# A third softmax buffer, with the softmax transposes and the value products one projection tile later

## What is computed

```
u = RMSNorm(h);  p = u @ w_in              # 28 column tiles of 128: rq rk rv rg dq dk dv, 4 heads each
# differential attention, head h, sequence b
logits = (q . k) * scale + bias            # two halves of 64 dims: two softmaxes, p0 and p1
a      = softmax(logits0) - lam * softmax(logits1)
out    = a @ v;  out = RMSNorm(out) * gain * (1 - lam_init)
# retention (second head group): scores * decay, times v, group norm, silu gate
h = h + concat(retention, attention) @ w_out
```

## Time and profile before

| what | before |
|---|---|
| median of 3 runs | 1997.98 us (1997.11 to 1999.52) |
| the profiled execution | 1998.23 us |
| its span in the trace | 1996.4 us, so 1.8 us lie around it |
| TensorE busy | 1955.0 us, 98% of the span, 8698 matmuls |
| VectorE, ScalarE, GpSimd busy | 732.5, 700.0, 856.0 us (37%, 35%, 43%) |
| mean granted TensorE clock | 0.993 of full speed |
| HBM traffic | 93 GB/s over the span |
| chain that ended last | TensorE 91%, VectorE 5%, issue 3%, ScalarE 1% |

### The profile page before, as it was taken

How to read it: one execution, slowest core, us unless ns; L and a number is a source line. 1 busy time by engine, 2 the same in 40 slices (tenths; PEclk the granted TensorE clock), 3 DMA queues, 4 the chain that set the end, 5 groups by cost and what they waited for, 6 DMA issues and landing times.

```text
span 1996.4 us, 24454 instructions
## 1 busy us (share of the span) xinstructions
PE 1955.0 (98%) x8698; PEld 1608.2 (81%) x8698; DVE 732.5 (37%) x1007; ACT 700.0 (35%) x997; POOL 856.0 (43%) x388
## 2 busy tenths in 40 slices
PE   9999999998899999999999999999989999999997
PEld 7888888886688888888878888888767888888886
DVE  4212332428575221212442124233485642122125
ACT  5322333445434322322532223234454243222224
POOL 4444443453334444444344444435433344444442
PEclk9999999999999999999999999999999999999999
DMA  4323232321122232222233222323211133222222
GB/s 149 130 98 114 96 110 90 100 97 62 49 68 86 97 103 96 95 95 93 91 103 117 95 95 95 105 82 109 85 53 53 53 106 105 96 95 95 95 95 74
DMA packets 54965, 186.00 MB, mean 93 GB/s; under 512 B 6440, under 2 KB 7976, under 8 KB 54860
## 3 DMA queue, kind: packets, MB, share of 16 engines
q1 hardware_dynamic: 53136, 181.61, 27.5%
q10 hardware_dynamic: 1724, 2.96, 0.5%
HBM read 182.44 MB, written 3.15 MB: 93 GB/s over the span
## 4 chain that ended last, share of the span: by engine, by line
PE 91%; DVE 5%; issue 3%; ACT 1%; DMA 0%; SPq 0%; DVEq 0%; ACTq 0%; POOL 0%; POOLq 0%
PE bank L457 20%; PE bank L459 20%; PE bank L458 20%; PE pair L457 7%; PE pair L459 7%; PE pair L458 7%; DVE neg_max L1184 1%; PE bank L479 1%; PE bank L475 1%; PE bank L476 1%; PE pair L672 1%; PE bank L687 1%; ACT s L933 1%; PE pair L506 1%; PE pair L501 1%
## 5 line engine op out<-in xcount | busy, mean ns | idle before, releaser
L415 POOL TENSOR_TENSOR w_lo<-raw,w_hi 128x1024 fp32r<-128x1024 f32 (+1 forms) x344 | 810.1, 2356 | 1088.4 <-ACT w_hi L745 1088.2
L745 ACT ACTIVATE w_hi<-raw 128x1024 fp32r<-128x1024 f32 (+1 forms) x344 | 355.5, 1034 | 680.3 <-PE bank L459 511.7
L457 PE MATMUL bank<-hg_hi,w_hi 128*128 128x512 f32 x1128 | 445.6, 395 | 0.0
L458 PE MATMUL bank<-hg_lo,w_hi 128*128 128x512 f32 x1128 | 440.6, 391 | 0.0
L459 PE MATMUL bank<-hg_hi,w_lo 128*128 128x512 f32 x1128 | 440.4, 390 | 0.0
L457 PE MATMUL bank<-a_hi,w_hi 128*128 128x512 f32 x768 | 299.5, 390 | 0.0
L458 PE MATMUL bank<-a_lo,w_hi 128*128 128x512 f32 x768 | 298.8, 389 | 0.0
L459 PE MATMUL bank<-a_hi,w_lo 128*128 128x512 f32 x768 | 298.8, 389 | 0.0
L457 PE MATMUL pair<-hg_hi,w_hi 128*128 128x512 f32 x656 | 255.2, 389 | 0.0
L458 PE MATMUL pair<-hg_lo,w_hi 128*128 128x512 f32 x656 | 255.2, 389 | 0.0
L459 PE MATMUL pair<-hg_hi,w_lo 128*128 128x512 f32 x656 | 255.2, 389 | 0.0
(11 more groups left out here) (181 smaller groups left out, 1480.7 us busy)
## 6 DMA issues: line engine op xcount, KB each, us to landing
raw<-in_w_gu SPq DMA_DIRECT2D x176, 512.0 KB, 3.3
raw<-in_w_dn SPq DMA_DIRECT2D x64, 512.0 KB, 3.2
raw<-in_w_p SPq DMA_DIRECT2D x56, 512.0 KB, 3.2
raw<-in_w_dn SPq DMA_DIRECT2D x32, 384.0 KB, 3.0
raw<-in_w_o SPq DMA_DIRECT2D x16, 512.0 KB, 3.2
out_y<-h SPq DMA_DIRECT2D x8, 256.0 KB, 2.1
h<-in_x ACTq DMA_DIRECT2D x4, 256.0 KB, 5.5
h<-in_x SPq DMA_DIRECT2D x4, 256.0 KB, 6.4
```

The lines of the kernel that those rows point to most:

```text
L415: pool.tensor_tensor(w_lo[:, s, 0:tiles, :].rearrange("p a b -> p (a b)"), raw[:, s % RAW, 0:n], w_hi[:, s, 0:tiles, :].rearrange("p a b - ...
L457: pe.matmul(out, w_hi[:, s, k, :], m_hi, start=first, stop=False)
L458: pe.matmul(out, w_hi[:, s, k, :], m_lo, start=False, stop=False)
L745: act.activation(w_hi[:, s, 0:tiles, :].rearrange("p a b -> p (a b)"), raw[:, s % RAW, 0:tiles * P], ACT.Copy).then_inc(hi_done, 1)
```

## The change

`turn_at` and `mixv_at` are raised by one step and `subln_at` with them. The softmax buffers become three: `s4` joins `soft` and `s1`, item n uses buffer n % 3, and the small arrays `neg_max` and `den` have three entries. The wait of DVE ahead of the bias is now for the transposes of item n - 3, which stand in the same step as before. The normalisation of item n stays one DVE step ahead of its transposes, so it moves by a step too. Because rv1 is written to half of `s4`, its take-over (step 19) now waits for the transposes of item 5 (step 19); items 2 and 5 are the ones held in `s4`. No instruction of an engine is added or removed but that one wait.

```diff
+SOFTS = 3
-def turn_at(n): return 13 + n
-def mixv_at(n): return 14 + n
-def subln_at(h): return 16 + 2 * h
+def turn_at(n): return 14 + n
+def mixv_at(n): return 15 + n
+def subln_at(h): return 17 + 2 * h
...
-        soft = [sb("soft", [P, 2, QT, SEQ])[:, :, :, :], s1[:, :, :].rearrange("p a (j k) -> p a j k", j=QT)]
+        soft = [sb("soft", [P, 2, QT, SEQ])[:, :, :, :], s1[:, :, :].rearrange("p a (j k) -> p a j k", j=QT),
+                s4[:, :, :].rearrange("p a (j k) -> p a j k", j=QT)]
...
-        neg_max = sb("neg_max", [P, 2, 2 * QT])
-        den = sb("den", [P, 2, 2 * QT])
+        neg_max = sb("neg_max", [P, SOFTS, 2 * QT])
+        den = sb("den", [P, SOFTS, 2 * QT])
...
-                        if n >= 2:
-
-                            dve.wait_ge(turn_done, at(turn_done, l, n - 1))
+                        if n >= SOFTS:
+
+                            dve.wait_ge(turn_done, at(turn_done, l, n - SOFTS + 1))
...
                     if (kind, hd) in (("rv", 2), ("rv", 3)):
 
                         dve.wait_ge(value_done, at(value_done, l, VALUES.index((kind, hd - 2)) + 1))
+                    elif (kind, hd) == ("rv", 1):
+
+                        dve.wait_ge(turn_done, at(turn_done, l, 6))
```

More of the change, by code:

```diff
@@ L623, in attention @@
                                 last = pe.transpose(turned[:, kt * SEQ + q0:kt * SEQ + q0 + P],
-                                                    soft[n % 2][:, 0, j, kt * P:(kt + 1) * P], ident[:, :])
+                                                    soft[n % SOFTS][:, 0, j, kt * P:(kt + 1) * P], ident[:, :])
                         last.then_inc(turn_done, 1)
@@ L931, in attention @@
                         for i in range(2 * QT):
-                            row = soft[n % 2][:, i // QT, i % QT, :]
-                            ins = act.activation(row, row, ACT.Exp, bias=neg_max[:, n % 2, i:i + 1],
-                                                 accum_out=den[:, n % 2, i:i + 1])
+                            row = soft[n % SOFTS][:, i // QT, i % QT, :]
+                            ins = act.activation(row, row, ACT.Exp, bias=neg_max[:, n % SOFTS, i:i + 1],
+                                                 accum_out=den[:, n % SOFTS, i:i + 1])
                         ins.then_inc(exp_done, 1)
@@ L1158, in attention @@
                         dve.wait_ge(exp_done, at(exp_done, l, n + 1))
-                        weights, sums = soft[n % 2], den[:, n % 2, :]
+                        weights, sums = soft[n % SOFTS], den[:, n % SOFTS, :]
                         dve.reciprocal(sums, sums).then_inc(dve_step, 1)
@@ L1177, in attention @@
                         dve.wait_ge(pair_done, at(pair_done, l, use + 1))
-                        if n >= 2:
-                            dve.wait_ge(turn_done, at(turn_done, l, n - 1))
-                        dve.tensor_tensor(soft[n % 2], pair[:, :, :].rearrange("p a (j k) -> p a j k", j=QT),
+                        if n >= SOFTS:
+                            dve.wait_ge(turn_done, at(turn_done, l, n - SOFTS + 1))
+                        dve.tensor_tensor(soft[n % SOFTS], pair[:, :, :].rearrange("p a (j k) -> p a j k", j=QT),
                                           windows(bias, n // 2), ALU.add).then_inc(pair_free, 1)
                         dve.wait_ge(pair_free, at(pair_free, l, use + 1))
-                        dve.tensor_reduce(neg_max[:, n % 2, :], soft[n % 2].rearrange("p a j k -> p (a j) k"), AX.X,
+                        dve.tensor_reduce(neg_max[:, n % SOFTS, :], soft[n % SOFTS].rearrange("p a j k -> p (a j) k"), AX.X,
                                           ALU.max, negate=True).then_inc(max_ready, 1)
```

## The result

The changed kernel takes 1978.89 us (median of 4 runs, 1977.57 to 1979.47); the ratio to the kernel before is 0.990, 95% interval 0.9884 to 0.9916. That is 19.1 us less than the 1997.98 us of before; 1976 us had been forecast, with a range from 1963 to 1987. The profiled execution took 1979.47 us, its span 1977.7 us. A fourth run of the kernel before took 4716.65 us and is left out of its median.

What follows compares the result with a forecast made beforehand. TensorE's waits and the half clock behind them were taken as the bound; 7.0 of 18.0 us a layer would stay, so 22 us off 1998.23 us gave 1976 us, with a range of 1963 to 1987 us.

Steps and rivals of the forecast that it cites:

- What bounds the kernel: TensorE, busy 98% of the span; with its instructions unchanged, only its waits and the half clock behind them can be saved.
- The sum of 36 us: Most to be won in two layers: 26.9 us of TensorE's attention waits plus 9.1 us lost at half clock.
- Part 1: Transposes, value product and head norm one step later: all 8 normalisations get one TensorE step more, about 8 us.
- part 3: Third buffer: no new wait for VectorE, as item n - 3's transposes precede the scores it awaits anyway.
- Part 2: Normalisations no longer stand right behind their exponentials, so VectorE's wait of 0.89 us goes.
- Part 4: The rv1 take-over waits for item 5's transposes: costs nothing, 0.4 us if VectorE were early.
- Part 5: First head norm from step 16 to 17: the 3.1 us Ln wait goes; VectorE's part falls between normalisations 4 and 5.
- The replay: Layer one's steps timed from the trace's durations: a 4.1 us wait at step 19; 1969 to 1981 us, chance 0.61.
- the sum: Losses left per layer: 0.4 + 0.7 + 4.1 + 1.8 = 7.0 us of 18.0; gain 22 us for both layers.
- Rival 1: VectorE just early enough, no wait at step 19: gain 17 us a layer, 1964 us; chance 0.14.
- Rival 3: The port decides: normalisations meet GpSimd in every step, gain only 6 to 8 us, 1984 us; chance 0.15.
- Rivals 2 and 4: 2: waits only move, 1996 to 1998 us, chance 0.05; 4: head norm meets GpSimd throughout, 2004 us, chance 0.05.

## Why the prediction was right, point by point

**What bounds the kernel** held: nothing but TensorE's waits and what follows them in clock changed. The sum of 36 us to be won was right in its first term and in kind for the second.

**Part 1, the later deadline,** and **part 3, the buffer:** shown by the two runs with one of them alone; neither is worth anything by itself: the buffer changes nothing, the shift costs 11 us. **Part 2:** the wait of the reciprocal for the exponentials is gone from all normalisations of the dense steps. **Part 4:** the new wait of the rv1 take-over costs nothing; VectorE gets there 2 us after those transposes have begun. **Part 5** weighs most, right in both its halves: the wait for the Ln went, and the head norm became the cause of the wait at step 19. Two experiments that only move or hurry the head norm take that wait away.

**The replay.** Product 14 starts 7.2 us behind product 13, as said. The trace lies 0.26 us later than that of before in this region; with this taken off, products 15 to 19 start at 467.6, 476.5, 485.0, 495.1 and 503.1 us, forecast were 467.5, 476.4, 484.9, 494.1 and 502.1. Items 0, 1, 2 and 4 met or missed GpSimd as written; items 3 and 5 each met one GpSimd instruction more. Product 23 starts at 543.4 (again less 0.26) instead of 541. Steps 23 to 30, where the prediction had looked for new waits, have none.

**Where the sum was off.** Forecast was a gain of 22 us, measured 19.1. Three terms of the sum were too small, per layer. The wait before the scores of item 6 was 1.45 instead of 0.7 us, because item 3 met two GpSimd instructions, where the replay had one. The second was the square of head 0, which starts at 488.67 together with the pair of L1173. The wait at step 19 was 4.55 instead of 4.1 us. Here normalisation 5 took 3.0 us (510.55 to 513.55), as its pair met the square of head 1 at 511.80; the replay had counted it free and given it 2.4 us, which is 0.4 us more than its own price of a free one. And the half clock behind that wait cost 2.5 (5.18 less 2.7) instead of 1.8 us. Together 1.9 us, against the 1.5 us a layer that are missing; the runs don't show where the other 0.4 us went.

**The rivals.** Rival 1 didn't happen, but it is what the two remedies make of the kernel: with one of them 1967 or 1965 us, near the 1964 us given for it. Rival 3 was half right: the port isn't what the change moves, but its remedy alone gave 13.9 us and the head norm's 11.9. Both go back to ScalarE's exponentials, which stand ahead of a short job and ahead of the weight split. The prediction had said so of the kernel before, and the changed kernel's rows show it still: the exponentials end at 484.33, the split follows at once, GpSimd's subtraction starts at 485.45 and normalisation 3 at 485.62. That this order places the meetings is read from the rows; no run moved the split by itself. Rivals 2 and 4 fell: the waits didn't just move, and nothing came near to 11 us of more delay.

## What to carry to other kernels

In a pipeline written out by hand, a later deadline can be worth nothing without a buffer that lets the producer run ahead, as here; test both parts alone before you believe in either. Then look at the order inside the helping engines: a factor of 1.3 us behind exponentials of 2 us on ScalarE cost as much as the whole change gave back. And where instructions of VectorE and GpSimd hold each other up, delay the one that isn't on the path: one wait on a semaphore, in two steps, gave the changed kernel 14 us. Such gains overlap, so measure them together too: with the factor moved first, holding GpSimd back in three steps gave 5.5 us.

## What was not expected

- Causes overlap. The change and the reordering on ScalarE gave 19 us each on the kernel before, together 31 us; with GpSimd held back, 36.5 us.
- The half clock isn't a fixed price of a wait. In the kernel before, waits of 2.99 us (510.93) and 3.01 us (1496.71, below) before the same transposes were followed by full clock in the first layer and met by half clock in the second. Behind the wait for the Ln at step 16 the half clock lasted 3.4 us in the first layer of the kernel before and 6.8 us in the same place when only ScalarE's factor was moved, with 5.65 us of TensorE's work in it. In one layer a wait of 6.8 us cost 1 us less of clock than one of 4.6 us, as more of the slow stretch fell into the idle time. If half of the work in such a stretch is counted as lost, these traces show between 0 and about 2.8 us a wait. The first line is of the kernel before, the second of the run with the factor moved:

```profile
1496.71 1.11 PE L623 MATMUL bank<-ident,s 128*128 128x128 f32 x4 [3.01 <-DVE s L1171]
...
491.30:498.20 6.90, 5.65 (x13) 4.47 (x14) 6.73 (x10) 3.54 (x6) 2.48 (x1) 0.51 0.24 76
```
